# Giving a kernel's first stages one set of buffers and loading the first tiles of the prompt's and the samples' attention in the stage ahead

## What is computed

```python
qa, ka, va, ga, qb, fb, ib, gb = jnp.split(h @ w_in, SPLITS_EVEN, axis=-1)
qa = rms_norm(qa.reshape(b, t, H_A, HD_A), qg)
ka = rms_norm(ka.reshape(b, t, H_A, HD_A), kg)
...
if past_k is None:
    oa = sb_prompt(qa, ka, va, sbb)
else:
    keys = jnp.concatenate([past_k, ka.astype(past_k.dtype)], axis=1)
    vals = jnp.concatenate([past_v, va.astype(past_v.dtype)], axis=1)
    oa = sb_attend(qa, keys, vals, p + jnp.arange(t), jnp.arange(p + t), sbb)
...
log_f = jnp.log(lb + (1.0 - lb) * jax.nn.sigmoid(fb32))
ob, s_new = gla_chunk_scan(q_b, k_b, v_b, log_f, s0, chunk)
mix = jnp.concatenate([oa.reshape(b, t, W_A) * jax.nn.silu(ga.astype(f32)),
                       ob.reshape(b, t, W_B) * jax.nn.silu(gb.astype(f32))], axis=-1)
return mix.astype(h.dtype) @ w_out, ka, va, s_new
```

## Time and profile before

| what | value |
| --- | --- |
| median of 3 runs | 2050.96 us (2048.17 to 2057.91) |
| the profiled execution's own time | 2047.05 us |
| its span, first to last instruction | 2044.8 us |
| even projection, by TensorE's matmuls | to 425.3 us |
| prompt's attention, TensorE | 438.1 to 670.8 us |
| samples' attention, TensorE | 679.8 to 798.5 us |
| HGRN2, TensorE | from 802.5 us |
| mean granted clock of TensorE, as a share of full | 0.959 |

### The profile page before, as it was taken

The page is one execution under the profiler, slowest core; times in us unless marked ns, Lnnn a source line. Parts: engine busy times, 40 slices in busy tenths (PEclk is TensorE's granted clock), DMA queues, the critical chain, the costliest instruction groups (busy, mean ns, idle before and its releaser), DMA issues. The chain is left out here.

```text
span 2044.8 us, 30859 instructions
## 1 busy us (share of the span) xinstructions
PE 1872.0 (92%) x11538; PEld 1508.4 (74%) x11538; DVE 849.4 (42%) x1472; ACT 521.2 (25%) x1133; POOL 594.3 (29%) x532
## 2 busy tenths in 40 slices
PE   6999999968887796796999999999999889999998
PEld 5788999955454553675889998888888757777776
DVE  3552000038788444873444443111000155656564
ACT  4220111037676322342420000000111232323231
POOL 3333222016666102413052222222331051213130
PEclk9999999979899887788999999999999989999999
DMA  4233222142430675516433233222224387565643
GB/s 152 79 108 115 92 96 107 46 138 63 134 114 21 177 237 171 151 59 207 151 113 96 85 98 99 90 90 86 91 92 147 100 236 249 188 207 158 202 135 139
DMA packets 210250, 261.71 MB, mean 128 GB/s; under 512 B 24261, under 2 KB 150917, under 8 KB 209861
## 3 DMA queue, kind: packets, MB, share of 16 engines
q1 hardware_dynamic: 155012, 201.63, 31.7%
q10 hardware_dynamic: 53104, 53.04, 8.0%
q0 software_dynamic: 2000, 5.25, 0.8%
HBM read 176.10 MB, written 81.40 MB: 126 GB/s over the span
## 5 line engine op out<-in xcount | busy, mean ns | idle before, releaser
L440 PE MATMUL odd_bank<-odd_w_hi,odd_h_hi 128*128 128x512 f32 x576 | 224.2, 389 | 0.0
L440 PE MATMUL odd_bank<-odd_w_lo,odd_h_hi 128*128 128x512 f32 x576 | 224.2, 389 | 0.0
L440 PE MATMUL odd_bank<-odd_w_hi,odd_h_lo 128*128 128x512 f32 x512 | 199.3, 389 | 0.0
L388 POOL CAST odd_w_hi<-ahead_raw 128x1024 fp32r<-128x1024 f32 x48 | 51.4, 1071 | 333.0 <-PE odd_bank L440 311.3
L440 PE MATMUL odd_bank<-odd_h_hi,odd_w_hi 128*128 128x362 f32 (+1 forms) x384 | 126.1, 328 | 1.8 <-POOL odd_w_lo L390 1.8
L440 PE MATMUL odd_bank<-odd_h_lo,odd_w_hi 128*128 128x362 f32 (+1 forms) x384 | 126.1, 329 | 0.0
L440 PE MATMUL even_bank<-even_h_hi,even_w_lo 128*128 128x362 f32 (+1 forms) x384 | 126.1, 328 | 0.0
L440 PE MATMUL even_bank<-even_h_hi,even_w_hi 128*128 128x362 f32 (+1 forms) x384 | 126.0, 328 | 0.0
L440 PE MATMUL even_bank<-even_h_lo,even_w_hi 128*128 128x362 f32 (+1 forms) x384 | 125.9, 328 | 0.0
L440 PE MATMUL odd_bank<-odd_h_hi,odd_w_lo 128*128 128x362 f32 (+1 forms) x384 | 125.1, 326 | 0.0
L440 PEld LDWEIGHTS odd_bank<-odd_w_hi,odd_h_hi 128*128 128x128 f32 x576 | 108.2, 188 | 22.4
(11 more groups left out here) (337 smaller groups left out, 4090.2 us busy)
## 6 DMA issues: line engine op xcount, KB each, us to landing
ahead_raw<-in_w_in_odd SPq DMA_DIRECT2D x48, 512.0 KB, 3.8
even_raw<-in_w_in_even SPq DMA_DIRECT2D x32, 512.0 KB, 3.8
k_page<-in_cache_k SPq DMA_DIRECT2D x64, 256.0 KB, 3.0
v_page<-in_cache_v SPq DMA_DIRECT2D x64, 256.0 KB, 3.0
rt_s<-in_state_ret SPq DMA_DIRECT2D x32, 512.0 KB, 5.3
v_tm<-odd_shared ACTq DMA_DIRECT2D x64, 128.0 KB, 2.0
g_tm<-odd_shared ACTq DMA_DIRECT2D x64, 128.0 KB, 1.9
ahead_place<-v_tm SPq DMA_DIRECT2D x32, 256.0 KB, 5.5
```

Of the source, the lines that this page charges most:

```text
L388: nc.gpsimd.tensor_copy(hi, r).then_inc(w_hi_done, 1)
L440: mm = pe.matmul(out, stationary, moving, start=(j == 0), stop=(j == len(pairs) - 1))
```

## The change

`FirstHead`, which holds the memory and semaphores of the first HGRN2 head, is now made before the even projection and handed to it. Its `place` grows from 6144 to 6272 elements a partition and takes the even projection's token tiles `x_in` and its `stage_fm`, later the prompt's tables, biases, first pair of queries, keys and values, later the samples' queries, keys and result. A new function `load_prompt` loads the prompt's first tiles at the end of SP's program of the even projection. The queries and keys of the samples are loaded by SP in the last pair of the prompt's attention. Three waits for landed stores move from a stage's end to a later place: `left_fm` to SP in the prompt's attention, and the two of `mix_left` to SP in the samples' attention and at the end of HGRN2. TensorE's wait for `rounded` goes behind its first transposes. `sums` moves from `first.place` to `pages.v[1]`.

```diff
-    if tag == "even":
-        project_in_now(nc, tag, None, *args)
-    else:
-        _held["odd"] = args
+    _held[tag] = args
...
-            if not even:
+            if even:
+
+                sp.wait_ge(turned, 2 * NT)
+                for i in range(NSTAGE):
+                    sp.wait_ge(left_tm[i], 32 * 3 * NT // NSTAGE + 16)
+                ahead.load_prompt(sp, *_held["prompt"], consts)
+            else:
...
-            for i in range(2):
-                act.wait_ge(left_fm[i], (16 if even else 48) * (fm // 2) + 16)
-            if not even:
+            if even:
+                assert 16 * (fm // 2) + 16 == LEFT_FM
+            else:
+                for i in range(2):
+                    act.wait_ge(left_fm[i], 48 * (fm // 2) + 16)
...
+    def load_prompt(self, sp, q_tm, k_tm, v_tm, bias_dram, consts):
+
+        tiles = lambda x: x[0:TP].rearrange("(t p) n -> p t n", p=P)[:, :, 0:P]
+        for i, x in enumerate((q_tm, k_tm)):
+            sp.dma_start(self.qk_prompt[:, i], tiles(x)).then_inc(self.qk_load, 16)
+        for dst, src in ((self.ident, consts["ident"]), (self.tri, consts["tri"]), (self.upper, consts["mask"]),
+                         (self.biases, bias_dram.to_broadcast([P, HA]))):
+            sp.dma_start(dst, src).then_inc(self.table_in, 16)
+        sp.dma_start(self.v_prompt, tiles(v_tm)).then_inc(self.v_load[0], 16)
...
-            for dst, name in ((ident, "ident"), (tri, "tri"), (mask, "mask")):
-                sp.dma_start(dst[:], consts[name]).then_inc(const_in, 16)
-            sp.dma_start(biases[:], bias_dram.to_broadcast([P, HA])).then_inc(const_in, 16)
-            load_qk(0)
-            load_v(0)
             load_v(1)
+            for x in first.left_fm:
+                sp.wait_ge(x, LEFT_FM)
...
+                else:
+                    for i, x in enumerate((q_tm[TP:T], k_samples)):
+                        sp.dma_start(first.qk_samples[:, i], x).then_inc(first.samples_in, 16)
             store_mix(NPAIR - 1)
-            sp.wait_ge(mix_left, 16 * NPAIR)
...
             pe.wait_ge(const_in, 64)
-            pe.wait_ge(rounded, 4)
             for i in range(4):
                 turn(0, i)
+            pe.wait_ge(rounded, 4)
...
-        NFIRST, NCONST = 16 * 5, 16 * 5
+        NFIRST, NCONST = 16 * 3, 16 * 5
...
-            for i, x in enumerate((q_tm[TP:T], k_tm)):
-                sp.dma_start(qk_in[:, i, :], x).then_inc(first_in, 16)
...
+            sp.wait_ge(mix_left, 16 * HA // 2)
             pages.load(sp, 1, keys=False)
+            sp.wait_ge(new_turned, 2)
             first.load(sp)
...
-            sp.wait_ge(mix_left, 16)
...
-            pe.wait_ge(first_in, NFIRST)
+            pe.wait_ge(first.samples_in, 32)
...
+            pe.wait_ge(first_in, NFIRST)
             pe.wait_ge(prep, 1)
...
             sp.wait_ge(mix_left, 32 * HB)
+            sp.wait_ge(first.mix_left, 16 * (HA // 2 + 1))
```

More of the change, by code:

```diff
@@ L210, in project_in_now @@
         nx = NX if even else 2
-        x_in = sb("x_in", [P, nx, D]) if even else ahead.in_projection()[3]
+        x_in = ahead.x_in if even else ahead.in_projection()[3]
         diag = sb("diag", [P, 2, P])
@@ L269, in project_in_now @@
         left_tm = [sem(f"left_tm{i}") for i in range(NSTAGE)] if even else ahead.left_tm
-        left_fm = [sem("left_fm0"), sem("left_fm1")]
+        left_fm = ahead.left_fm if even else [sem("left_fm0"), sem("left_fm1")]
         eps_set = sem("eps_set")
@@ L939, in __init__ @@
         sem = lambda n: nc.alloc_semaphore(f"first_{n}")
-        self.place = sb("place", [P, 6 * 8 * P])
+        self.place = sb("place", [P, NX * D + 2 * T])
+        self.x_in = self.place[:, 0:NX * D].rearrange("p (s n) -> p s n", s=NX)
+        self.stage_fm = self.place[:, NX * D:NX * D + 2 * T].rearrange("p (s t) -> p s t", s=2)
+        self.qk_prompt = self.place[:, 0:2 * TP].rearrange("p (a c n) -> p a c n", a=2, c=TP // P)
+        self.v_prompt = self.place[:, 2 * TP:3 * TP].rearrange("p (c n) -> p c n", n=P)
+        self.ident, self.tri, self.upper = (self.place[:, 3 * TP + i * P:3 * TP + (i + 1) * P] for i in range(3))
+        self.biases = self.place[:, 3 * TP + 3 * P:3 * TP + 3 * P + HA]
+        self.qk_samples = self.place[0:TS, 4 * TP:4 * TP + 2 * WA].rearrange("t (i n) -> t i n", i=2)
+        self.mix_samples = self.place[:, 5 * T:5 * T + WA // P * TS].rearrange("p (c t) -> p c t", t=TS)
+        self.left_fm, self.v_load = ([sem(f"{n}{i}") for i in range(2)] for n in ("left_fm", "v_load"))
+        self.table_in, self.qk_load, self.samples_in, self.mix_left = (sem(n) for n in ("table_in", "qk_load", "samples_in", "mix_left"))
         self.f, self.k, self.q, self.qd, self.e = (self.place[:, i * T:(i + 1) * T] for i in range(5))
@@ L1012, in attend_prompt @@
         later, at, spot = pages.v[1][:].rearrange("p u n -> p (u n)"), 0, []
-        for n in (P, P, P, 8 * P, TP, NW * NQ):
+        for n in (8 * P, TP, NW * NQ, NX * NQ):
             spot.append(later[:, at:at + n])
             at += n
-        ident, tri, mask, v_odd, gate, w = spot
-        w = w.rearrange("p (x n) -> p x n", x=NW)
-        at, spot = 0, []
-        for n in (2 * 8 * P, 8 * P, NX * NQ):
-            spot.append(first.place[:, at:at + n])
-            at += n
-        qk_in = spot[0].rearrange("p (a c n) -> p a c n", a=2, c=8)
-        v = [x.rearrange("p (c n) -> p c n", c=8) for x in (spot[1], v_odd)]
+        v_odd, gate, w, sums = spot
+        w, sums = (x.rearrange("p (x n) -> p x n", n=NQ) for x in (w, sums))
+        ident, tri, mask, biases, qk_in = first.ident, first.tri, first.upper, first.biases, first.qk_prompt
+        v = [first.v_prompt, v_odd.rearrange("p (c n) -> p c n", n=P)]
         qk_hi, qk_lo = ([sb(f"{n}{i}", [P, 2, TP], F32R) for i in range(2)] for n in ("qk_hi", "qk_lo"))
@@ L1027, in attend_prompt @@
         ident_r, mask_r = sb("ident_r", [P, P], F32R), sb("mask_r", [P, P], F32R)
-        biases = sb("biases", [P, HA])
-        sums = spot[2].rearrange("p (x n) -> p x n", x=NX)
         k_hi, k_lo = sb("k_hi", [P, ND, NQ], F32R), sb("k_lo", [P, ND, NQ], F32R)
@@ L1050, in attend_prompt @@
         summed, w_done, pv_done = sem("summed"), sem("w"), sem("pv")
-        mixed, mix_left = sem("mixed"), sem("mix_left")
+        mixed, mix_left = sem("mixed"), first.mix_left
         block = ctx.enter_context(nc.Block())
@@ L1312, in attend_samples @@
         spot = sb("spot", [P, 2, WA])
[L1313 removed]
+        qk_in = first.qk_samples
         qT, kT_new = sb("qT", [P, HP, TS]), sb("kT_new", [P, HP, TS])
         q_now = [sb(f"q_now{i}", [P, HP, 2, 4 * LS]) for i in range(2)]
[L1317 removed]
+        gate, mix = sb("gate", [P, HP, TS]), first.mix_samples
         k_page, v_page, k_in, v_in = pages.k, pages.v, pages.k_in, pages.v_in
@@ L1338, in attend_samples @@
         soft_step, keep_step = sem("soft_step"), sem("keep_step")
-        outputs, mined, mix_left = sem("outputs"), sem("mined"), sem("mix_left")
+        outputs, mined, mix_left = sem("outputs"), sem("mined"), first.mix_left
         block = ctx.enter_context(nc.Block())
-        NFIRST, NCONST = 16 * 5, 16 * 5
+        NFIRST, NCONST = 16 * 3, 16 * 5
         NTURN = NS // 4
@@ L1632, in hgrn @@
 def hgrn(nc, q_fm, sig_fm, v_tm, gate_fm, bounds, out_gain, state_in, state_prompt, state_samples, mix_fm, consts):
-    neg_fm = _held.pop("negative")
+    neg_fm = _held["negative"] = nc.dram_tensor("sig_neg_fm", (WB, T), F32).ap()
+    q_tm, k_tm, v_attend, _, _, _, bias_dram, *_ = _held["attend"]
+    _held["prompt"] = q_tm, k_tm, v_attend, bias_dram
     with nc.cleanup_on_exit(), ExitStack() as ctx:
         first = FirstHead(nc, ctx, q_fm, sig_fm, neg_fm, bounds, consts["level_mask"])
+        project_in_now(nc, "even", first, *_held.pop("even"))
         attend_now(nc, first, *_held.pop("attend"))
```

34 lines of the change are left out of this document (16 added, 18 removed).

## The result

The changed kernel takes 2038.34 us (median of 17 runs, 2031.61 to 2050.64), the kernel before 2050.96 us (17 runs beside them, 2043.49 to 2057.91): a ratio of 0.9936, 95% interval 0.9921 to 0.9951. So 13 to 16 us are gone; forecast were 14.75. The profiled execution took 2033.7 us with a span of 2031.5, against 2047.05 and 2044.8.

A forecast was written before the change was run, and what follows sets the result against it. TensorE, busy for 92% of the span, bounds the kernel, so mostly its standing time can go. 10.3 + 2.9 + 1.55 = 14.75 us off the profiled 2047.05 gives 2032.3, or 2036 us for a median; range 2030 to 2042.

The forecast's parts named there:

- Even projection to prompt: First boundary: without the store wait and with loads issued early, the prompt's first logits come 10.3 us earlier.
- The price of nothing for the 1.7 MB: Seven prompt loads, 1.7 MB, moved into the even projection were taken to cost nothing there, of up to 6 us.
- one sign of being wrong: The step is wrong if the even stage takes longer than 425.3 us to TensorE's last matmul.
- Prompt to samples: Second boundary: no store wait and two fewer loads in SP's queue bring VectorE's first page copy 2.9 us earlier.
- The price of a boundary: Time from a last store's issue end to the next stage's first instruction without a wait, taken as 1.5 us.
- Samples to HGRN2: Third boundary: without the wait for the samples' store, HGRN2 opens 1.55 us earlier.
- The first rival: TensorE's clock stays up at the prompt's start: 2.8 us more gained, 2033 us; chance 0.15.
- that rival's other branch: The clock falls and comes back later than before, losing as much at first and second place together: 2039 us.
- the objection in the prediction: Against the clock staying up at the prompt's start: two pauses follow each other closely there.
- the starts that don't move: Stage openings hang on something other than the last store's landing; only loads count, 9.4 us, 2041.6 us; chance 0.10.
- the collision: Early loads delay the even stage's stores, up to 6 us come back: 8.75 us gained, 2042 us; chance 0.05.
- the slower one: TensorE stays at the lower clock in the prompt's attention, 53 us over the whole stage, about 2086 us; chance 0.03.

The follow-up runs named there:

- e1: Changed kernel with ScalarE again waiting at the even projection's end until both buffers of stage_fm have landed; single execution 2033.6 us.
- e2: Changed kernel with the prompt's first seven loads issued again at the start of the prompt's stage; median 2043.19 us, ratio 0.9948 to the kernel before.
- e7: Changed kernel with the prompt's three table roundings moved to VectorE and ScalarE's table load put behind its roundings of turned tiles; single execution 2038.14 us.
- after_again: The changed kernel once more, without any edit; median 2035.14 us of 6 runs, ratio 0.9922 to the kernel before.
- e3: Changed kernel with SP's waits for the last mix store put back at the ends of the prompt's and samples' attention; single execution 2038.46 us.
- e4: Changed kernel with the samples' queries and keys loaded again at the start of the samples' stage, first on SP; single execution 2049.01 us.
- e6: Changed kernel with VectorE's wait for masks, tables and gate moved behind its first page copy; run twice, 2027.23 us once, then median 2029.73 us, ratio 0.9915.
- e5: Changed kernel with 22 more transposes on TensorE to fill its second pause at the prompt's start; single execution 2034.65 us.
- e9: Changed kernel with the edits of e6 and e7, and no load of biases and ones in the samples' start; median 2031.07 us, ratio 0.9912.
- e6_const_late: The first of the two runs of e6, changed kernel with VectorE's wait for masks, tables and gate moved later; single execution 2027.23 us.

## Why the prediction was right, point by point

Forecast were 2036 us, 2030 to 2042, and faster with a chance of 0.80; measured 2038.34.

**Even projection to prompt: right.** The opening was put at 427.6 and came at 427.39; the logits were put 10.3 us earlier and came 10.62 earlier. e1 and e2 show that it takes both halves, the wait (2.3 us) and the loads (7.0 us), and e7 that ScalarE's table load and roundings are the bound behind them, as the sum assumed. The price of nothing for the 1.7 MB holds. By the letter one sign of being wrong came: the last even matmul ends at 425.36 us and not by 425.3, 0.11 us later than before. But that 0.11 us is there from 99 us on, long before the loads are issued at 338.85, and the last 600 matmuls take 112.28 us in both kernels.

The Trainium skill, ScalarE: Activation LUTs, section "What ACT_TABLE_LOAD costs", puts a drain of about 1.38 us beside the load; an estimate with it has 8.9 us here. The row above has 1.30 us from the start of the load to the next operation, and the runs gave 10.6: no drain shows in this place.

**Prompt to samples: the mechanism right, the term too small.** 2.9 us were forecast, 3.9 came (12.01 to 8.10 us from the store's issue end to the first copy; 4.7 by after_again, since the gate landed 0.75 us late in the first profile). Both parts were undersized. The price of a boundary was taken as 1.5 us from the odd projection; here it is 0.92 us, so the wait was worth 2.35 and not 1.75 us (2.29 by e3). And the loads that left SP's queue moved the gate's issue by 2.33 us and not 1.17: e4 gives 1.36 to them, and the rest is the slow issue in the trace of before, which the sum took for a fixed cost. That the gate stays what is late next was right (e6).

**Samples to HGRN2: right.** 1.55 forecast, 1.62 measured.

**The clock: forecast to be as before, and so nearly.** That was the assumption without a term of its own. The first rival, that it stays up, did not happen: in the changed kernel's profile it was low for 17.1 us behind the first logits, before for 13.7 us (in 445.6 to 459.2). What came is nearer to that rival's other branch, a clock that falls and comes back later, which had 2039 us. By the 0.22 us of the table the longer stretch explains 0.75 of the 1.2 us that the prompt gave back; the rest stays open.

The Trainium skill, TensorE: Matmul & The Clock Gate, section "Why this matters for your kernels", says that short gaps between bursts leave the upper level on; I gave that rival weight from it and from the row before the retention. Here a short gap was not safe. In nine traces the first pause is 2.22 us, as in the changed kernel; in six of them (after_again, e3, e5, both of e6, e7) the clock fell 2.9 to 3.2 us behind the last even matmul, while the transposes ran and ahead of the second pause, and in three (the first profile, e4, e9) 7.1 to 7.5 us behind it, after both. So the objection in the prediction, that two pauses follow each other closely, had the outcome right, but it isn't what brought the clock down in those six. And the row before the retention, the other ground for that rival, was one execution. The same pause, 3.27 to 3.29 us, stands in all twelve traces. In four (before, e6_const_late, e7, e9) the clock stayed up behind it, and in eight, the changed kernel's among them, it fell. The retention of the changed kernel, whose first matmul starts at 1611.91 us:

```profile
1614.00:1615.00 1.00, 1.00 (x7) 0.77 (x6) 0.00 (x0) 0.99 (x3) 0.05 (x1) 0.50 0.75 163
```

**The sum** was 14.75, the profiles differ by 13.35: +0.3 at the first place, +1.0 at the second, +0.1 at the third, and -2.8 that went back in the prompt and the stages behind it, most of it with the clock. So the closeness of the total is in part luck: errors of both signs met. Of the other rivals, the starts that don't move fell with e1 and e3, the collision with the 112.28 us that end the even stage in every trace, and the slower one did not come: its nearest case is e4, whose prompt spent some 70 us at the lower level (0.15 x 2 x 233.72) and took 5 us longer than the changed kernel's, where 53 had been put on the whole stage at that level. In the chances a sum is off: 0.67 and 0.15 make 0.82 and not 0.81, so the 0.80 for faster lies 0.02 under its two cases, and the 0.17 for no change 0.02 above its two.

## What to carry to other kernels

A wait for stores to land at a stage's end held up the next stage by 1.6 to 2.4 us here; move such a wait to the first instruction that needs the landed data or the freed buffer. But at the first place the larger part of the opening was the stage's own first loads (7.0 against 2.3 us), so find memory in which they can land during the stage ahead, and then look again at what is late next, which here was a wait placed ahead of work that didn't need it. Where a total scatters by more than the gain, read each edit as a distance between two events of its own trace, and put the granted clock beside any total before believing it.

## What the runs showed of the hardware that was not expected

- The price of a stage's boundary, from the end of the last issue to the first instruction, is not one number: 0.92 us behind SP's store at the prompt's end, 1.16 behind ScalarE's at the even projection's end, 1.43 behind SP's at the samples' end, 1.45 before the retention. Each repeats within 0.02 us from run to run, where the edits leave it alone, with one exception: before the retention it is 1.80 and 1.79 us in e7 and e9, whose edits lie far ahead of it. Why they differ was not tried.
- The scatter of this kernel's totals goes with the clock, if not run by run (2038.34 us at 0.953, 2038.46 at 0.959). In its 17 runs the quickest, 2031.61 us, has a mean granted clock of 0.961 and the slowest, 2050.64 us, of 0.949, with the same instructions. That difference is 2 x (0.051 x 2050.64 - 0.039 x 2031.61) = 51 us more at the lower level, for 19 us of time.
- The same pauses of TensorE end at the upper level in one execution and at the lower in another: the pause in the odd projection at 1047 to 1051 us left the clock at 1.00 before and at 0.50 after (at 0.50 in seven of the twelve traces), that before the retention in eight of twelve, and behind the same pause of 2.22 us at the prompt's start the fall came 2.9 to 7.5 us after the last even matmul.
- One issue on SP's queue can take 1.0 us more than the same issue in another execution (the ones' load, 1.39 and 0.43 us, above); a term that is read from one such row carries that.
